# A mixer and top-4-of-32 MoE step on one core: gate/up products in two phases over the same weight places, with the next round's gather between them

## The reference

```python
def moe_ffn(h, router_w, router_b, w_gu, b_gu, w_down, b_down):
    ...
    def expert_block(args):
        x_blk, e = args
        gu = x_blk @ w_gu[e] + b_gu[e]
        gate = jnp.minimum(gu[:, :D_FF], SWIGLU_LIMIT)
        up = jnp.clip(gu[:, D_FF:], -SWIGLU_LIMIT, SWIGLU_LIMIT)
        glu = gate * jax.nn.sigmoid(SWIGLU_ALPHA * gate)
        return ((up + 1.0) * glu) @ w_down[e] + b_down[e]
    ...
```

## Time and profile before

| | us |
|---|---|
| median of 3 runs (1209.75 to 1211.62) | 1210.2 |
| the profiled execution, whole | 1211.84 |
| its span, first to last instruction | 1210.1 |
| TensorE busy | 1026.0 (85%) |
| VectorE busy | 399.3 (33%) |
| ScalarE busy | 168.7 (14%) |
| GpSimd busy | 126.9 (10%) |
| granted TensorE clock, mean | 0.955 |
| moved by DMA | 463.66 MB, mean 383 GB/s |

### The profile page before, as it was taken

One profiled execution on the slowest core, in us unless ns is written; L12 is line 12 of the kernel. 1 busy time (PEld: TensorE's weight loads), 2 busy tenths in 40 slices (PEclk: granted clock), 3 DMA queues, 4 the chain that ended last, 5 costly groups with the idle time before them and its releaser, 6 DMA issues.

```text
span 1210.1 us, 31803 instructions
## 1 busy us (share of the span) xinstructions
PE 1026.0 (85%) x11930; PEld 494.7 (41%) x11931; DVE 399.3 (33%) x1157; ACT 168.7 (14%) x459; POOL 126.9 (10%) x323
## 2 busy tenths in 40 slices
PE   4899998988899779898579898998756899999864
PEld 4678777645333224333123334333312233334321
DVE  1045593866123212233123232231211232222313
ACT  2242314143000001001000001000000000001002
POOL 0041003101001101001000010010100000010100
PEclk9899998998999999999989999999988899999997
DMA  9936938799999999999999996999999999999996
GB/s 339 346 140 222 343 116 244 291 335 398 427 428 427 429 428 429 427 428 429 428 430 427 430 415 290 431 427 429 428 429 428 429 428 428 429 426 430 427 429 278
DMA packets 77830, 463.66 MB, mean 383 GB/s; under 512 B 11531, under 2 KB 31185, under 8 KB 53146
## 3 DMA queue, kind: packets, MB, share of 16 engines
q1 hardware_dynamic: 70479, 460.88, 92.9%
q10 hardware_dynamic: 7315, 2.27, 0.9%
HBM read 455.56 MB, written 7.57 MB: 383 GB/s over the span
## 4 chain that ended last, share of the span: by engine, by line
PE 64%; DMA 19%; DVE 7%; SPq 4%; issue 4%; DVEq 1%; ACT 1%; ACTq 0%
PE psum L665 25%; PE psum L684 14%; DMA weights<-in_w_gu 12%; PE psum L1018 4%; PE psum L640 4%; DMA work<-in_w_down 4%; SPq L905 3%; PE psum L1268 2%; DMA weights<-in_w_ada 2%; PE psum L617 2%; PE psum L634 2%; PE psum L1023 2%; PE psum L973 1%; DMA work<-l_blocks 1%; DVE work L2396 1%
## 5 line engine op out<-in xcount | busy, mean ns | idle before, releaser
L665 PE MATMUL psum<-weights,work 128*32 128x512 f32 x2928 | 346.0, 612 | 92.2 <-DMA weights<-in_w_gu 45.5
L665 PEld LDWEIGHTS psum<-weights,work 128*32 128x32 f32 x2928 | 92.6, 111 | 315.0 <-issue 241.8
L684 PE MATMUL psum<-weights,work 128*32 128x256 f32 x2624 | 167.0, 407 | 34.2 <-DVE work L2410 32.1
L2396 DVE STREAM_TRANSPOSE work<-psum 128x256 f32<-128x256 f32 x53 | 23.9, 450 | 420.8 <-PE psum L665 418.1
L684 PEld LDWEIGHTS psum<-weights,work 128*32 128x32 f32 x2624 | 85.7, 116 | 109.7 <-issue 56.7
L1814 ACT ACTIVATE work<-work x53 | 22.1, 416 | 501.1 <-DVE work L2400 501.1
L2420 DVE STREAM_TRANSPOSE work<-work 128x288 f32<-128x288 f32 x53 | 25.4, 478 | 201.5 <-PE psum L640 201.5
L617 PE MATMUL psum<-work 128*32 128x257 f32 (+1 forms) x1296 | 88.2, 385 | 3.2 <-ACT work L1811 3.2
L1018 PE MATMUL psum<-work,weights 128*128 128x288 f32 x320 | 81.6, 412 | 0.0
L1018 PEld LDWEIGHTS psum<-work,weights 128*128 128x128 f32 x320 | 60.3, 191 | 17.9 <-issue 2.0
L617 PEld LDWEIGHTS psum<-work 128*32 128x32 f32 (+1 forms) x1296 | 37.5, 109 | 67.2 <-issue 58.4
(11 more groups left out here) (401 smaller groups left out, 909.4 us busy)
## 6 DMA issues: line engine op xcount, KB each, us to landing
weights<-in_w_gu SPq DMA_DIRECT2D x112, 2048.0 KB, 37.4
weights<-in_w_down SPq DMA_DIRECT2D x48, 2048.0 KB, 39.6
work<-in_w_gu SPq DMA_DIRECT2D x16, 2048.0 KB, 34.0
work<-in_w_down SPq DMA_DIRECT2D x16, 2048.0 KB, 43.4
weights<-in_w_ada SPq DMA_DIRECT2D x12, 2048.0 KB, 11.9
weights<-in_w_in SPq DMA_DIRECT2D x6, 2048.0 KB, 13.7
weights<-in_w_out SPq DMA_DIRECT2D x2, 2048.0 KB, 8.7
out<-weights SPq DMA_DIRECT2D x8, 512.0 KB, 8.5
```

Of the source, the lines that this page charges most:

```text
L665: last = mm(bank(GB)[SLOTS * n:SLOTS * n + SLOTS, :].rearrange("p (a x) -> p a x", a=4), xTm[:, k, :], gu[:, k % 2, n], start=k == 0, stop ...
L684: last = mm(bank(YB)[SLOTS * q:SLOTS * q + SLOTS, 0:QW], hT[:, k, :], dn[:, k % 4, QW * q:QW * q + QW], start=k == 0, stop=k == KT - 1)
L2396: v.transpose(features, of_slots[0]).then_inc(s["hid_step"], 1)
```

## The change

The gate/up product of a round becomes two products over the same four places. In the first phase all eight k steps run over the gate columns (256 in each of the four groups) into bank 2; then comes the gather for the next round; in the second phase the eight k steps run over the up columns into bank 3. The waits for landing stand in the first phase. `gu_read` is signalled in the second phase, at k = 1, 3 and 5, and `gu_ps` at its end; the end of the first phase has a signal of its own, `gate_ps`.

The down product now writes bank 2 instead of bank 3 (`YB`), so TensorE waits for `y_sb` before a round's gate phase (the last down product of the experts before has been moved out), and for `xTa` of the expert's last round before the down loop. VectorE starts with gate's part on `gate_ps`; it transposes the first half of x when the gather is done and k = 3 of the up phase has read the old half, then up on `gu_ps`, then the second half of x. ScalarE reads bank 2 instead of 3 for y. Nothing else is touched.

```diff
--- before.py
+++ after.py
@@ -604,7 +604,7 @@
             return mixer_slots[n].at(0, 4, D) if n in mixer_slots else W.at(SLOT_W * n, 4, D)
 
         def experts_pe(pe, mm, tr):
-            XB, GB, YB, TB, RB = 0, 2, 3, 4, 5
+            XB, GB, UB, YB, TB, RB = 0, 2, 3, 2, 4, 5
 
             def gather_by(sel, cols, first=False):
 
@@ -655,19 +655,24 @@
 
                 with pe.Fori(first, end) as i:
 
+                    pe.wait_ge(s["y_sb"], first)
                     pe.wait_ge(s["xTa"], i)
-                    for k in range(KT):
-                        if k % 2 == 0:
-                            gu = slot_gu(landed(k // 2)).rearrange("p j (a n x) -> p j n a x", a=4, n=NQ)
-                        if k == KT // 2:
-                            pe.wait_ge(s["xTm"], i)
-                        for n in range(NQ):
-                            last = mm(bank(GB)[SLOTS * n:SLOTS * n + SLOTS, :].rearrange("p (a x) -> p a x", a=4), xTm[:, k, :],
-                                      gu[:, k % 2, n], start=k == 0, stop=k == KT - 1)
-                        if k in (1, 3, 5):
-                            last.then_inc(s["gu_read"], 1)
-                    last.then_inc(s["gu_ps"], 1)
-                    gather(i + 1)
+                    for part in range(2):
+                        out = bank((GB, UB)[part])
+                        for k in range(KT):
+                            if k % 2 == 0:
+                                at = landed(k // 2) if part == 0 else slot_of(r, k // 2)[0]
+                                gu = slot_gu(at).rearrange("p j (a n x) -> p j n a x", a=4, n=NQ)
+                            if part == 0 and k == KT // 2:
+                                pe.wait_ge(s["xTm"], i)
+                            for n in range(NQ):
+                                last = mm(out[SLOTS * n:SLOTS * n + SLOTS, 0:QW].rearrange("p (a x) -> p a x", a=2), xTm[:, k, :],
+                                          gu[:, k % 2, n, 2 * part:2 * part + 2], start=k == 0, stop=k == KT - 1)
+                            if part and k in (1, 3, 5):
+                                last.then_inc(s["gu_read"], 1)
+                        last.then_inc(s["gu_ps" if part else "gate_ps"], 1)
+                        if part == 0:
+                            gather(i + 1)
 
                 if of:
                     bias_products()
@@ -675,6 +680,7 @@
                 with pe.Fori(first, end) as i:
 
                     pe.wait_ge(s["y_sb"], i)
+                    pe.wait_ge(s["xTa"], end)
                     pe.wait_ge(s["hid"], i)
                     hT = hid_all[:, 0, :].rearrange("p (k t) -> p k t", k=KT)
                     for k in range(KT):
@@ -1819,7 +1825,7 @@
                     act.copy(hid_all[:, 0, :], hid_next[:, round_behind(i, first), :].rearrange("p r n -> p (r n)"))
                     act.wait_ge(s["xg_ps"], 1)
                     act.wait_ge(s["y_st"], i)
-                    fn(y_sb, bank(3)[:, 0:QW], ACT.Identity, scale=gslot[:, round_of(i, first)]).then_inc(s["y_sb"], 1)
+                    fn(y_sb, bank(2)[:, 0:QW], ACT.Identity, scale=gslot[:, round_of(i, first)]).then_inc(s["y_sb"], 1)
             rounds = act.value_load(cum_i[0:1, NE:NE + 1], min_val=2, max_val=257)
 
             fn(st[0:1, 14:15], st[0:1, 13:14], ACT.Sqrt)
@@ -2381,7 +2387,7 @@
 
             v.wait_ge(s["cum"], 8)
             v.wait_ge(s["gbT"], 1)
-            of_slots = [bank(2)[:, 256 * t:256 * t + 256].rearrange("p (a f j) -> p a j f", a=2, j=4) for t in range(2)]
+            of_slots = [bank(2 + t)[:, 0:QW].rearrange("p (a f j) -> p a j f", a=2, j=4) for t in range(2)]
             features, part = hidg.rearrange("p (a j t) -> p a j t", a=2, j=4), hidg.rearrange("p (k t) -> p k t", k=KT)
             v.wait_ge(s["rank_b"], 1)
 
@@ -2392,15 +2398,19 @@
                 bias = [bguT[:, KT * t:KT * t + KT, bass.ds(expert, 1)].to_broadcast([P, KT, SLOTS]) for t in range(2)]
                 with v.Fori(first, end) as i:
                     kept = hid_all[:, round_of(i, first), :].rearrange("p r n -> p (r n)")
-                    v.wait_ge(s["gu_ps"], i)
+                    v.wait_ge(s["gate_ps"], i + 1)
+                    v.wait_ge(s["y_sb"], first)
                     v.transpose(features, of_slots[0]).then_inc(s["hid_step"], 1)
                     v.wait_ge(s["hid_step"], i * 5 + 1)
                     tt(kept.rearrange("p (k t) -> p k t", k=KT), part, bias[0], ALU.add).then_inc(s["hid_step"], 1)
                     v.wait_ge(s["hid_step"], i * 5 + 2)
                     ts(kept, kept, LIMIT, None, ALU.min).then_inc(s["g_ready"], 1)
+                    v.wait_ge(s["xg_ps"], i + 1)
+                    v.wait_ge(s["gu_read"], i * 3 + 2)
+                    x_half(0).then_inc(s["xTa"], 1)
+                    v.wait_ge(s["gu_ps"], i)
                     v.transpose(features, of_slots[1]).then_inc(s["hid_step"], 1)
-                    v.wait_ge(s["xg_ps"], i + 1)
-                    x_transposes()
+                    x_half(1).then_inc(s["xTm"], 1)
                     v.wait_ge(s["hid_step"], i * 5 + 3)
                     tt(part, part, bias[1], ALU.add).then_inc(s["hid_step"], 1)
                     v.wait_ge(s["hid_step"], i * 5 + 4)
```

## The result

| | before | after |
|---|---|---|
| median of 11 runs each, us | 1211.0 (1206.51 to 1213.82) | 1217.47 (1212.27 to 1222.29) |
| the profiled execution, whole / its span | 1211.84 / 1210.1 | 1218.03 / 1216.2 |
| TensorE busy | 1026.0 (85%) | 1034.6 (85%) |
| matmul records | 11930 | 15322 |
| granted TensorE clock, mean | 0.955 | 0.939 |

The ratio of the times is 1.005, with a 95% interval of 1.0034 to 1.0066: about 6 us slower. The forecast was 1.4 us slower with a range up to 1215.0; the median lies beyond it. The two spans differ by 6.1 us as well, so the traces hold what has to be explained.

The account below looks back on a forecast made before the run. The prediction took the weight stream as the bound, except where TensorE alone sets the pace before the queue's restart. It summed -0.6 + 0 + 2.0 = +1.4 us on the median 1210.2: 1211.6, range 1208.3 to 1215.0.

Parts of the forecast that it names:

- chain (a) to (d): (a) stream to expert 13's last gate/up landing; (b) TensorE alone until the queue restarts; (c) 92 places streamed; (d) the end.
- The ring at expert 1: Expert 1's place 1, released later behind the gather, would not leave the transfer queue empty: 0, at most 1 us.
- the queue needs it at 302.9: Expert 1's place 1: need counted 63 places back from 616.17, plus one for the transfer; release put at 300.3 to 302.6.
- The ring at expert 18: Place releases just after the queue's restart: no lost transfer, 0; margins worked out for experts 19 and 20 only.
- TensorE alone: Expert 13's last gate/up landing to the queue's restart, experts 13 to 15: -0.6 us, bounds -2.0 and +1.4.
- 3.59 per phase: Each gate or up phase of 64 half-width records takes 3.59 us, as such records do in the down product.
- rival 5: Half-width phases take 3.44 us, not 3.59, in nine rounds: -2.7 us more, 1205.8 in all; chance 0.05.
- Rival 4: A 0.9 us wait per round stays, first half of x being late: 5.4 us, total 1217 to 1219; chance 0.03.
- The tail: Expert 32's last gate/up landing to its down product's second half: one low-clock spell of 1.7 us, +2.0 us.
- Rival 2: Expert 32's first down half also runs at low clock: 1.7 us more, +3.1 in all, 1213.3; chance 0.34.
- Theory A: Set up for the follow-ups: the loss is three places, experts 1, 16 and 32, while the rounds win.
- theory B: Set up for the follow-ups: two phases cost something everywhere, by later releases or VectorE, and show at the places seen.

Follow-up runs that it names:

- first_gather_last: The changed kernel with expert 1's gather alone moved behind its up phase; ratio 1.0053 to the kernel before.
- split_but_1: The late split with expert 1 alone put back to the changed kernel's two phases, gather between; 1.0002 of the kernel before.
- split_but_16: The late split with expert 16 alone put back to the changed kernel's two phases, a loop turn written out; 1.0004 of the kernel before.
- gather_last: The changed kernel with every gather moved behind the up phase; ratio 1.0080 to the kernel before.
- warm_last: The changed kernel with idle products behind k = 1, 3 and 5 of expert 32's gate phase, a loop turn written out; 1.0065 of the kernel before.
- split_but_32: The late split with expert 32 alone put back to the changed kernel's two phases, a loop turn written out; 1.0020 of the kernel before.
- the late split: The changed kernel with gate and up together up to k = 5, the gather between gate and up of k = 6, 7; 0.9972 of before, again 0.9976.
- three_experts: The changed kernel with expert 1's gather last, experts 16 and 32 in one pass, two loop turns written out; transfer stretch 446.02 us, time ratio not given.
- both_ends: The changed kernel with expert 1's gather last and expert 32 in one pass, a loop turn written out; 0.23% slower than the kernel before.
- last_one_pass: The changed kernel with expert 32's gate and up in one pass, gather behind, last loop turn written out; 1.0047 of the kernel before.

## Why the prediction was wrong

The chain (a) to (d) was right, and so was what the prediction said that an edit can touch: (b), (d), or a queue that runs dry elsewhere. The failure was in the last of these, with two smaller ones in sizes.

1. **The ring at expert 1, forecast 0, measured +3.6; the main failure.** The step was "the queue needs it at 302.9", set against a release at 300.3 to 302.6. The release was inside its bounds: 302.2 in the changed kernel, 301.8 on the old scale, since the gather ran low for all of its 2.95 us where the sum had 2.10 and the low clock only as an option. The need was wrong, by two steps. It was counted back from 616.17, a time of use, without the delay between a place's last byte and its use. From 616.17 until the queue was empty the trace of before moved 23.56 places' bytes, and 24 places were still to come behind this one, so its last byte was there 0.44 of a place, 2.1 us, before its use. The need was therefore near 300.7, and the changed kernel's bytes did stop at 300.3, 299.9 on the old scale. And the release was set against the need as if it were the first byte: the prediction's own 0.40 from release to issue and 1.05 to the first byte were not added. With them even 302.9 would have been missed by up to 1.2 us at the low clock. "At most 1 us as the bound" had no row behind it. first_gather_last takes 3.0 of the 3.6 away and split_but_1 brings all of it back.

   The delay from last byte to use is not one number. Of the last place, used at 1193.60, the last byte was there about 1.1 us before: the trace had moved 92 places' bytes by 1192.5, and then the rate falls to 224 GB/s. (741.4 + 92 x 4.89 = 1191.3 would make it 2.3, but up to 745 only 1.26 MB had been moved, 2.9 us at the full rate, so that the full rate counts from 742.1 and not from 741.4.) The Trainium skill ("DMA: Bandwidth & Descriptors", section "Anatomy of one DMA — SWDGE (gpsimd) path") gives a fixed cost of about 2.0 us per transfer, most of it behind the last byte; that is for transfers issued by GpSimd, these are issued by SyncE, and the 1.1 to 2.1 us here are of that size.

2. **The ring at expert 18, forecast 0; the stretch measured +1.9, and 0.9 of that is shown to come from here.** "Behind the restart the ring is tightest" was right and then worked out for the places of experts 19 and 20. For expert 18's place 1 nothing was worked out. The sum takes three lines: the restart queues two places, 9.8 us; expert 16 starts its product 745.83 - 741.75 = 4.1 us behind the restart, and reads place 1 in its up phase 6.0 us later; the issue is due at 10.1 to 10.4 and the queue empty at 9.8. Even at the full clock it was late. Experts 19 and 20 held, as forecast, and with more room: expert 19's place 1 was issued at 778.13, and what was queued lasts to about 741.75 + 1.05 + 8 x 4.89 = 781.9. split_but_16 brings the dip back alone, with 1.1 us of bytes; gather_last, where the issue is in time, has neither dip nor loss of bytes. The rest of the +1.9 is not tied to this place, see below.

3. **TensorE alone, forecast -0.6, measured -2.6.** The sign was right. The term "3.59 per phase" was mis-sized: the phases take 3.46; why the same number of such records takes 3.59 in the down product was not tried. That was rival 5's price at a chance of 0.05, and its ground against ("of the same form") was weak. Expert by expert: 13 from landing to down product +1.64 (15.75 against 14.11; forecast +2.09), 14 from first product to down product -0.86 (forecast -0.37), 15 -3.53 (forecast -2.33). Rival 4, the wait that stays, did not occur: no round of expert 15 waits. Experts of one round went through in 10.80, not 11.15, by the same term.

4. **The tail, forecast +2.0, measured +2.9.** The mechanism, a spell at 1.2 GHz once the slack is gone, was right and warm_last shows it. At the full clock 0.87 + 1.55 + 3.46 + 2.3 + 1.73 = 9.9 just meets the transfer's 9.9, so every low microsecond counts. The size was off because the spell was taken as long as a wide quarter, 1.7. It did not end with the records it started with: it went on through the gather and into the up phase: by the starts of the rows 0.84 + 1.33 + 0.69 = 2.9 us lost. Rival 2 gave 3.7 and put the second spell in the down product's first half, which here ran at the full clock; in warm_last, split_but_1 and split_but_32 it ran low.

Together +3.6 - 2.6 + 1.9 + 2.9 is 5.8, with 0.4 ahead of the router and -0.1 at the end 6.1, the spans' difference. Theory A holds for the first stretch, for the tail and for the bytes lost at the restart. For the two phases' price elsewhere the late split says little, since it reads only the first two places and the last of each expert twice and releases them early. Two-phase kernels without a dip at the restart still have 0.7 us (gather_last) and 1.2 us (three_experts, before its last place) more in the transfer stretch, so theory B is not refuted for an amount of that size.

**What stays open.** About 1 us of the transfer stretch in the changed kernel is not in the bytes. Summed over windows from the restart on, the changed kernel has moved 0.3 to 0.4 MB less than before, 0.9 us at 428 GB/s, while its places land 1.9 to 2.0 us late, from 117 us behind the restart to the end. In split_but_16 the bytes lag by 1.2 us and the landings by 2.3, in both_ends by 1.0 to 1.2 and 2.7, in last_one_pass by 0.9 to 1.1 and 2.9, in three_experts, without a dip, by 0.3 and 1.2. The Trainium skill ("DMA: Bandwidth & Descriptors", section "Queues, rings and completion order") says that one transfer is split over up to 16 rings, and that the end of a later transfer says nothing about an earlier one's part on the other engines. So a landing could hang on the slowest engine while the rate is the mean of all. No view here shows single DMA engines, so this is a candidate and not a finding. A second candidate is the loop turn written out: last_one_pass and warm_last have 1.0 and 0.6 us more in this stretch than the changed kernel, both_ends 1.0 more than first_gather_last, split_but_32 1.3 to 1.6 more than the late split. In last_one_pass and both_ends, though, the landings are late from 120 us behind the restart on, long before the written-out turn. A kernel with that edit alone would tell. What the landings cost beyond the bytes is not explained.
